# Hosted modulation pieces: one copy and one fold for each batch of up to ten

## The reference, cut to what matters

```python
for i in range(DEPTH):
    m_l = (jax.nn.silu(c) @ mod_w + mod_b)[:, None, :]
    m_c = jax.nn.silu(c_ctx) @ mod_w + mod_b
    sh1_l, sc1_l, g1_l, sh2_l, sc2_l, g2_l = jnp.split(m_l, 6, axis=-1)
    ...
    p_lat = _ada(x, norm1, sh1_l, sc1_l) @ w_in
    ... even_mixer or odd_mixer ...
    x = x + g1_l * (o_l.astype(x.dtype) @ w_out)
    x = x + g2_l * _sq_relu_mlp(_ada(x, norm2, sh2_l, sc2_l), mlp_w1, mlp_w2)
```

## Time and profile before

| | us |
|---|---|
| time, median of 3 runs | 2031.5 |
| lowest and highest | 2029.34, 2032.51 |
| span of the profiled execution | 2027.8 |

### The profile page before, as it was taken

The page is one execution under the profiler, slowest core; times in us unless marked ns, Lnnn a source line. Parts: engine busy times, 40 slices in busy tenths (PEclk is TensorE's granted clock), DMA queues, the critical chain, the costliest instruction groups (busy, mean ns, idle before and its releaser), DMA issues. The chain is left out here.

```text
span 2027.8 us, 42258 instructions
## 1 busy us (share of the span) xinstructions
PE 1853.9 (91%) x18096; PEld 1620.7 (80%) x18096; DVE 1252.8 (62%) x2170; ACT 858.4 (42%) x1588; POOL 291.0 (14%) x341
## 2 busy tenths in 40 slices
PE   7999877776899999999999799999889999889997
PEld 5787546656669888888978689999589999679997
DVE  4574785575567532543675778745668756667753
ACT  4321676345334221221435445534555345554432
POOL 0202204215131000003001321012030012021001
PEclk8999988979999999999999889999999999989998
DMA  9752840020243232323420166554136455225543
GB/s 314 204 179 83 276 161 4 4 64 5 68 143 101 87 104 83 104 83 104 125 83 1 49 197 191 188 188 155 56 108 195 155 188 187 84 84 186 187 150 102
DMA packets 249005, 255.04 MB, mean 126 GB/s; under 512 B 6914, under 2 KB 247187, under 8 KB 248691
## 3 DMA queue, kind: packets, MB, share of 16 engines
q1 hardware_dynamic: 239214, 242.85, 37.1%
q10 hardware_dynamic: 8740, 8.51, 1.3%
q0 software_dynamic: 864, 0.98, 0.3%
HBM read 251.28 MB, written 1.05 MB: 124 GB/s over the span
## 5 line engine op out<-in xcount | busy, mean ns | idle before, releaser
L529 DVE TENSOR_TENSOR RING_rounded<-RING,SC_rounded 128x1024 fp32r<-128x1024 f32 (+2 forms) x390 | 462.2, 1228 | 225.4 <-ACT SC_rounded L522 225.1
L549 PE MATMUL bank<-OT_rounded,SC_rounded 128*128 128x256 f32 (+1 forms) x1808 | 575.8, 318 | 14.5 <-DVE HT_rounded L1115 6.8
L550 PE MATMUL bank<-HT_rounded,SC_rounded 128*128 128x256 f32 (+1 forms) x1808 | 570.4, 316 | 0.0
L551 PE MATMUL bank<-OT_rounded,RING_rounded 128*128 128x256 f32 (+1 forms) x1808 | 568.9, 315 | 0.0
L522 ACT ACTIVATE SC_rounded<-RING 128x1024 fp32r<-128x1024 f32 (+2 forms) x390 | 372.6, 1006 | 327.6 <-DMA RING<-in_l_mlp_w 183.6
L549 PEld LDWEIGHTS bank<-OT_rounded,SC_rounded 128*128 128x128 f32 x1808 | 343.4, 190 | 44.9 <-DVE HT_rounded L1115 7.6
L551 PEld LDWEIGHTS bank<-OT_rounded,RING_rounded 128*128 128x128 f32 x1808 | 342.7, 190 | 25.4
L550 PEld LDWEIGHTS bank<-HT_rounded,SC_rounded 128*128 128x128 f32 x1808 | 343.1, 190 | 21.7
L549 PE MATMUL bank<-PT_rounded,SC_rounded 128*128 128x256 f32 (+1 forms) x896 | 277.5, 310 | 4.9 <-DVE RING_rounded L529 4.9
L550 PE MATMUL bank<-PT_rounded,SC_rounded 128*128 128x256 f32 (+1 forms) x896 | 276.5, 309 | 0.0
L551 PE MATMUL bank<-PT_rounded,RING_rounded 128*128 128x256 f32 (+1 forms) x896 | 275.9, 308 | 0.0
(11 more groups left out here) (570 smaller groups left out, 2807.4 us busy)
## 6 DMA issues: line engine op xcount, KB each, us to landing
RING<-in_l_mlp_w SPq DMA_DIRECT2D x64, 1024.0 KB, 5.2
RING<-in_w_ffn_in SPq DMA_DIRECT2D x44, 1024.0 KB, 5.1
RING<-in_l_mod_w SPq DMA_DIRECT2D x32, 1024.0 KB, 5.5
RING<-in_l_w_in SPq DMA_DIRECT2D x25, 1024.0 KB, 6.4
RING<-in_w_ffn_out SPq DMA_DIRECT2D x16, 768.0 KB, 4.3
RING<-in_w_in SPq DMA_DIRECT2D x10, 1024.0 KB, 5.3
RING<-in_w_ffn_out SPq DMA_DIRECT2D x16, 640.0 KB, 3.9
PT<-in_l_mod_w SPq DMA_DIRECT2D x8, 1024.0 KB, 9.9
```

What stands on the lines that cost most here:

```text
L529: net.nc.vector.tensor_tensor(low, whole, net.high4(s, m)[:, 0:self.w.kts[s], :].bitcast(F32), ALU.subtract).then_inc(self.split_ready, 1)
L549: net.nc.tensor.matmul(bank[:, tokens], high, x_high, start=start, stop=False)
L550: net.nc.tensor.matmul(bank[:, tokens], high, x_low, start=False, stop=False)
L551: return net.nc.tensor.matmul(bank[:, tokens], low, x_high, start=False, stop=stop)
```

## The change

Several pieces now add into the same bank before one copy and one fold. The two conditions lie in a new tile `net.COND` of 8 x 50 columns, zero elsewhere, at columns 18 and 19. `window(i)` is a slice of 32 columns of it in which the conditions stand at columns 2i and 2i+1. With the slice of place i as the stationary operand, piece i of a batch adds its sums to rows 2i and 2i+1 of each group of 32 and zeros to the others. `start` is set on the batch's first matmuls only, `stop` on its last. The constant of `fold` grows from 2 to 20 columns, of which a fold uses two for each piece.

`plan` cuts the pieces of a stage into equal batches of up to ten: 9 and 10 in attention, and 6, 3 and 4 in the others. `copy` and `fold` now go by batches. In attention the copy of the first batch stands on ScalarE's queue at the unit after the one that hosts its last piece, and `exps(0)` and `exps(1)` have no copy ahead of them. In the other three stages the one copy is the last thing on ScalarE. `biases` takes the place of `bias` in the four hosting stages. Its columns are ordered otherwise, so it issues two adds for each batch and layer: six in attention (batch 1 has pieces of both layers), two in each other stage. The first stage keeps its own code, and `bias` for its pieces 8 to 15. The constants after the fold's move by 18 columns.

```diff
+MOD_BATCH = 10
+C_OVER = C_FOLD + 2 * MOD_BATCH
...
+        self.COND = sb("COND", [P, KT, 32 + 2 * (MOD_BATCH - 1)])
...
-        self.c = net.SC[:, 8440:8696].rearrange("p (t m) -> p t m", m=32)
+        self.c = self.window(0)
...
-    def add(self, pe, n, first):
-
-        if n > first:
-            self.fold(pe, n - 1, first)
-        s = n % SLOTS
+    def window(self, i):
+
+        at = 2 * (MOD_BATCH - 1 - i)
+        return self.net.COND[:, :, at:at + 32]
+
+    def plan(self, first, last):
+
+        count = -(-(last + 1 - first) // MOD_BATCH)
+        ends = [first + (last + 1 - first) * n // count for n in range(count + 1)]
+        self.done += len(self.batches)
+        self.batches = [range(a, b) for a, b in zip(ends, ends[1:])]
...
+    def add(self, pe, n):
+
+        b, s = self.batch(n), n % SLOTS
+        slots = self.batches[b]
+        if n == slots[0] and b:
+            self.fold(pe, b - 1)
         pe.wait_ge(self.net.ring_loaded[s], 16 * (n // SLOTS + 1) + self.base[s])
         for i in range(2):
             for j in range(4):
                 kt, group = 4 * i + j, slice(32 * j, 32 * j + 32)
-                last = self.nc.tensor.matmul(self.sums[group, :], self.c[:, kt, :],
-                                             self.net.RING[:, s, SW * kt:SW * kt + SW], start=(i == 0), stop=(i == 1))
+                last = self.nc.tensor.matmul(self.sums[group, :], self.window(n - slots[0])[:, kt, :],
+                                             self.net.RING[:, s, SW * kt:SW * kt + SW], start=(n == slots[0] and i == 0),
+                                             stop=(n == slots[-1] and i == 1))
         last.then_inc(self.summed, 1)
 
-    def copy(self, act, n):
-        act.wait_ge(self.summed, n + 1)
-        if n:
-            act.wait_ge(self.folded, n)
+    def copy(self, act, b):
+        act.wait_ge(self.summed, self.batches[b][-1] + 1)
+        if b:
+            act.wait_ge(self.folded, self.count(b - 1))
         act.activation(self.rows, self.sums, ACT.Copy).then_inc(self.copied, 1)
 
-    def fold(self, pe, n, first):
-        pe.wait_ge(self.copied, n + 1)
+    def fold(self, pe, b):
+        pe.wait_ge(self.copied, self.count(b))
+        count = 2 * len(self.batches[b])
         for m in range(2):
-            last = self.nc.tensor.matmul(self.columns[:, 2 * (n - first) + m, :], self.rows[:, P * m:P * m + P],
-                                         self.net.const(C_FOLD, 2), start=True, stop=True)
+            last = self.nc.tensor.matmul(self.batch_columns[:, b, m, 0:count], self.rows[:, P * m:P * m + P],
+                                         self.net.const(C_FOLD, count), start=True, stop=True)
         last.then_inc(self.folded, 1)
...
+    def biases(self, dve):
+
+        half = self.ALL // 2
+        dve.wait_ge(self.folded, self.count(len(self.batches) - 1))
+        for slots in self.batches:
+            b = self.batch(slots[0])
+            for some in (range(slots[0], min(slots[-1] + 1, half)), range(max(slots[0], half), slots[-1] + 1)):
...
-            pool.memset(mod.c, 0.0).then_inc(zeroed, 1)
+            pool.memset(net.COND[:, :, :], 0.0).then_inc(zeroed, 1)
...
-            mod.copy(act, ahead[0])
             exps(0)
-            mod.copy(act, ahead[1])
             exps(1)
-            mod.copy(act, ahead[2])
             for u, (h, q) in enumerate(units):
                 k0 = first_key(q) * P
-                for n in hosted[u - 1] if u else ():
-                    mod.copy(act, n)
+                for b, slots in enumerate(mod.batches):
+                    if u and slots[-1] in hosted[u - 1]:
+                        mod.copy(act, b)
...
-            mod.copy(act, first_slot)
             kr = mem.kr.rearrange("p t c n m -> p (t c) n m")
             act.wait_ge(cum_ready, 1)
             act.activation(kr[:, :, 1, :], flat(mem.cum), ACT.Exp, scale=-DECAY).then_inc(exped, 1)
-            mod.copy(act, first_slot + 1)
             act.activation(flat(mem.bd), flat(mem.cum), ACT.Exp, scale=DECAY).then_inc(exped, 1)
-            mod.copy(act, first_slot + 2)
             act.wait_ge(cum_ready, 2)
             act.wait_ge(rate_used, 1)
             act.activation(kr[:, :, 0, :], flat(mem.sig), ACT.Exp, scale=-DECAY).then_inc(exped, 1)
```

More of the change, by code:

```diff
@@ L418, in __init__ @@
         self.columns = net.ps[7][:, 256:512].rearrange("p (t n) -> p t n", n=2)
+        self.batch_columns = net.ps[7][:, 256:512].rearrange("p (b m n) -> p b m n", m=2, n=32)
+        self.batches, self.done = [], 0
         self.base = list(net.ring_base)
@@ L465, in bias @@
+    def bias(self, dve, first, last):
+        dve.wait_ge(self.folded, last + 1)
+        count, layer = 2 * (last + 1 - first), 2 * first // 48
         at = COL[f"l{layer}_mod_b"] + 2 * first - 48 * layer
-        return self.nc.vector.tensor_tensor(self.net.MOD[:, 2 * first:2 * last + 2, :], self.columns[:, of:of + count, :],
+        return self.nc.vector.tensor_tensor(self.net.MOD[:, 2 * first:2 * last + 2, :], self.columns[:, 0:count, :],
                                             self.net.PAR[:, at:at + count].unsqueeze(2).to_broadcast([P, count, 2]),
@@ L2701, in _ @@
                 for n in hosted[u]:
-                    mod.add(pe, n, first_slot)
+                    mod.add(pe, n)
             weigh(len(units) - 1)
-            mod.fold(pe, last_slot, first_slot)
+            mod.fold(pe, len(mod.batches) - 1)
         @st.scalar
@@ L2739, in _ @@
                     act.activation(f, f, ACT.Copy, scale=net.DER[:, 14 + t:15 + t]).then_inc(damped, 1)
-            for n in hosted[-1]:
-                mod.copy(act, n)
+            mod.copy(act, len(mod.batches) - 1)
         @st.vector
@@ L2783, in _ @@
             nc.vector.tensor_copy(net.OT[:, 3, :], net.ps[6][:, :])
-            for some in ((first_slot, 23), (24, last_slot)):
-                mod.bias(dve, (first_slot, last_slot), *some)
+            mod.biases(dve)
 def load_log_exp(net, act):
@@ L3104, in _ @@
             act.activation(mem.far, mem.far, ACT.Exp, scale=-DECAY)
-            for n in range(first_slot + 2, last_slot + 1):
-                mod.copy(act, n)
+            mod.copy(act, 0)
         @st.vector
@@ L3439, in _ @@
                                  stop=True).then_inc(gate_ready, 1)
[L3440 to L3441 removed]
+                mod.add(pe, first_slot + t)
+            mod.fold(pe, len(mod.batches) - 1)
         @st.scalar
@@ L3453, in _ @@
                                                        for t in range(4)])
-            for n in range(first_slot, last_slot + 1):
-                mod.copy(act, n)
+            mod.copy(act, 0)
         @st.vector
```

47 lines of the change are left out of this document (27 added, 20 removed).

## The result

The changed kernel took 2014.4 us (median of 6 runs, 2009.4 to 2017.4), the kernel before 2030.2 (6 runs, 2028.8 to 2032.5). The ratio is 0.9926, with a 95% interval of 0.9913 to 0.9939: 15 us faster, where I had forecast 9.8. The profiled execution took 2013.0 us with a span of 2011.1, so some 1.9 us lie outside the span. Against the 2027.8 of the earlier trace rows the span is 16.7 us shorter.

A forecast was written before the change was run, and what follows sets the result against it. It saw TensorE busy in most of a 2027.8 us span. Attention 5.8, rwkv_prepare 3.2, rwkv_back_decay -0.1 and rwkv_finish 0.9 made 9.8 us, taken off the median 2031.5: 2021.7 us, range 2017.0 to 2027.5.

The forecast's parts named there:

- the term for attention's start: Start of attention: three adds without copies and folds between let score(2) start earlier; gain 3.2 us, between 2.0 and 3.7.
- what lies outside the hosting stages: Stages that host no pieces: no gain or loss counted, 0 us.
- since the clock fell at about the second add: Attention's start: reason for taking score(2) at 205.4, between 204.9 and 206.6, with the first add beginning at 201.7.
- my upper bound: Attention's start: score(2) at 204.9 at the earliest, from 201.7 + 3 x 1.07; gain at most 3.7 us.
- Attention's units: Attention after its start: fewer folds on TensorE, 0.64 us per four units; gain 3.0 us, between 1.5 and 5.5.
- The biases: End of attention: four more bias adds on VectorE cost 0.4 us, between 0.2 and 0.8.
- `rwkv_prepare`: Copies no longer hold up ScalarE's last wide exponential, 2.6 us earlier; stage gains 3.2 us, between 2.0 and 3.7.
- Chunks 0: Stage behind rwkv_prepare: a worse clock phase costs about 1 us, but counted as 0 since the clock is already low.
- rival (b): Clock phase: three stages behind a host start with longer half-clock stretches, 2 us each; 3.8 us net, 2027.7; chance 0.09.
- `rwkv_back_decay` and `rwkv_finish`: First loses 0.1 us for a bias add; second gains 0.9 us from an earlier last fold, between 0 and 1.0.
- Rival (c): Slower loads: shifted slices load three times as long, an add takes some 1.8 us for 1.07; 2041 us; chance 0.05.
- Rival (a): Filler only: start at half clock, half the folds hidden, prepare at its lower bound; 4.6 us net, 2026.9; chance 0.10.

The follow-up runs named there:

- a_again: The changed kernel run once more, unaltered, for a second profile; ratio 0.9946 to the kernel before.
- e4_batched_pad64: The changed kernel with an unused tile of 64 bytes per partition behind CONST; ratio 0.9930 to the kernel before.
- g_all: All batches as in the changed kernel, but folded columns written in the old order, with the old bias adds; ratio 0.9941 to the kernel before.
- x_exps_first: The kernel before with exps(0) and exps(1) moved ahead of the copies of pieces 16 and 17 on ScalarE; ratio 1.0002.
- b_again: The kernel before run again, unchanged, for a second profile; ratio 0.9993.
- g_start: The kernel before with the changed kernel's layout and only attention's three pieces ahead (16 to 18) batched; ratio 0.9954.
- e1: The kernel before with the changed kernel's memory layout and nothing else; ratio 0.9999.
- e2: The kernel before with an unused tile of 64 bytes per partition behind CONST, so only addresses move; ratio 0.9987.
- g_prep: The kernel before with the changed kernel's layout and only the six pieces of rwkv_prepare batched; ratio 0.9990.
- x_warm_start: The kernel before with four unused identity matmuls on TensorE between score(1) and the add of piece 16; ratio 0.9988.
- h_warm: g_all plus unused identity matmuls at the ends of rwkv_prepare (three) and rwkv_back_decay (four); 2011.7 us, ratio 0.9924 to the kernel before.

## Why the prediction was wrong, point by point

**The whole.** The four kernels with all batches and no filler (changed, a_again, e4_batched_pad64, g_all) have ratios of 0.9926, 0.9946, 0.9930 and 0.9941. Weighted by their intervals that is 0.9936, a gain of 13.0 us give or take 1.5 if the four are taken as independent (a_again and g_all share their runs of the kernel before), for 9.8 forecast. The 15.8 us between the first two medians are at the high end: in the second set the changed kernel's median was 1.6 us higher (2016.0 for 2014.4) and that of the kernel before 2.4 us lower (2027.8 for 2030.2). Two steps of the prediction failed: the term for attention's start, 3.2 us, was too small, and what lies outside the hosting stages was put at 0.

**Attention's start: the first step that failed.** I had 3.2 us, bounds 2.0 and 3.7. In the pair of profiles the turn went from 12.3 to 7.4 us, 4.9. By the table it takes 12.7 us on average in the seven kernels with neither its batch nor the filler, and 8.1 in the six with it: 4.6 us. The mechanism was right: TensorE's waits for copies go, and ScalarE's order is worth nothing (x_exps_first). The size was wrong in three places. First, "since the clock fell at about the second add": I kept that fall for the changed kernel and took 3.7 us from the first add to score(2). It took 2.73, at full clock. Second, my upper bound was three adds at full clock, but it added 1.07 us three times, 3.2 us, where adds that follow one another take 2.80 us for three. Third, it ended at score(2). From there to the transposition it was 1.2 us at half clock and is 0.6 at full.

At full clock on both sides (b_again against the changed kernel) the turn gains only 10.2 - 7.4 = 2.8 us; the other 1.8 of the 4.6 come from the clock. The clock fell during the turn in six of those seven profiles, for 5.5 to 10.0 us, and in two of the six with the batch (g_start, e4), for 3.4 us each; in those two the turn took 9.3, in the four others 7.4 to 7.5. The Trainium skill ("TensorE: Matmul & The Clock Gate", part 1) says that activity releases the throttle. I had read that against the change alone, as filler work taken away. Here the folds were followed by waits, and the adds now stand closer together. That this is what keeps the clock up agrees with the counts and with the 2.80 us for three adds, but no run shows it apart from chance: the kernel before kept the clock up once as well.

**Attention's units: right in mechanism, somewhat large in size.** Four units take 14.7 us for 15.4, 0.66 less where I had 0.64, and VectorE is what is late, as said. Units with the end: 59.9 us on average in six unbatched kernels (before, b_again, e1, e2, x_exps_first, g_prep) and 57.8 in the three with the new bias adds: 2.1 for 3.0 - 0.4 = 2.6. Without e1 and x_exps_first, whose units took some 1.5 us longer than the others', it is 1.6, and in the first pair 1.8. The biases cost 0.26 (0.55 for six adds, 0.29 for two in the earlier trace rows), not 0.4, so the folds gave 1.9 to 2.4, not 3.0.

**`rwkv_prepare`: right in this pair, somewhat larger on average.** 3.3 us for 3.2. The wide exponential comes 2.7 us earlier in the stage (26.6 for 29.3 us; forecast 2.6), and the fold is what is late, 0.62 us, with VectorE next. The average over all profiles without a filler here is 46.3 us unbatched against 42.2 batched: 4.1. The length again goes with the clock. Where 13.7 of the stage's first 16.5 us run at half clock, it is 47.4 (b_again, e1) against 44.2 (g_all), and otherwise 44.8 to 46.5 against 41.6 to 41.7.

**Chunks 0: the term set to zero.** 104.4 us on average behind an unbatched prepare, 105.3 behind a batched one: 0.9 us given back. This is rival (b) at half its price. The clock is what differs: the stage has 13 us at half clock on average where prepare is batched, and 4.4 where it is not. The longer idle time ahead that the rival named shows in the stage's head (5.1 to 5.9 us at half clock in four of those five, 3.0 to 3.6 in seven of the eight others, 5.8 in the eighth). The larger part lies in stretches later in the stage, and why the clock falls there is open. Single profiles of one side differ by up to 3.8 us here, so the safer figure is that of prepare and chunks 0 together: 150.7 against 147.5 us, 3.2.

**`rwkv_back_decay` and `rwkv_finish`: right.** +0.1 for +0.1, and -0.9 for -0.9.

**Rival (c)** is refuted: loads out of shifted slices take 117 ns for 118, an add 1.07 us. **Rival (a)** too: the start ran at full clock in four of the six kernels with its batch, and the folds were on the path.

**The sum.** By the averages: 7.1 (attention, 72.6 in the six kernels without its batches or the filler against 65.5 in the five with both) + 4.1 - 0.9 - 0.1 + 0.9 = 11.1 us in the stages that the change reaches. Of the 1.3 us above the forecast, the start gives 1.7 (12.7 against 7.8 in these five), the units -0.4, prepare 0.9, chunks 0 -0.9. Up to the 13.0 us of the times 1.9 are left.

**Outside: the second step that failed.** I counted the phase of the clock at 0, and the fast end of the range, 2017.0, left 1 us for it beyond the sum of my upper bounds (13.5 us, or 2018.0). The first stage and what lies behind the first MLP's start gave 7.3 us in the pair. This was not the chance of these two executions alone: the second profiles, a_again and b_again, differ there by 6.9 us. Two things show in it.

The first is the layout. The first stage took 196.4 to 197.6 us in the four kernels with the tiles at their old places (before, b_again, x_exps_first, x_warm_start) and 193.8 to 196.2 in the ten where they are shifted. With the same 10.2 us at half clock in it, it is 196.6 against 195.2. From the first MLP's start to the first scan the four took 527.4 to 528.5 us with 10.1 to 11.9 of them at half clock, and four of the ten 525.9 to 527.2 with 11.7 to 14.5. The second MLP takes back 1 us (256.5 to 257.0 against 257.4 to 259.4). An estimate from these is 2 us in all, and the times of e1_layout and e2_pad64 (0.2 and 2.6 us) allow that.

The second is the clock. The other six of the ten kernels (e2, g_prep, changed, a_again, e4, h_warm) had only 6.3 to 7.2 us at half clock between the first MLP's start and the first scan, and took 521.3 to 523.8 us. The first profile of the kernel before was at half clock for 73.6 us behind the first MLP's start, that of the changed kernel for 55.4. This makes the last column fall in two groups, 1451.0 to 1452.2 and 1455.1 to 1456.3. Both occur with batches (four short, one long) and without (three short, six long), so batching does not fix the group. Whether it makes the short one more likely is open: with 14 profiles, chance can't be excluded. The clocks of all runs bear on it. Among runs of one kernel, a mean granted clock that is higher by 0.01 goes with a time that is some 8 us shorter (188 runs). Runs of the five kernels that batch attention's start without a filler had a mean clock of 0.968 to 0.969, the runs of the kernel before in the first two groups 0.966; by that slope, an estimate, 2 to 3 us of the gain go with the clock, attention's own share of it included.

## What to carry to other kernels

Ask of each short matmul group behind a wait not only what it costs, but what clock it runs at, and whether that follows from the wait. Where a wait in a dense stretch goes, the gain can be larger than the wait, since more of the stretch then runs at full clock (here 4.6 us on average for 2.8 at full clock on both sides); what is gained ahead of a stage can be partly given back in it, by the clock. And where a stage's length varies by 2 us from one execution to the next, take the stage's price from several profiles of several kernels, and give the range room on both sides: one pair of profiles put 7.3 us, nearly half the difference, into stretches whose work the change leaves alone. A change that adds a tile also moves others: run the old kernel with the new layout before a difference elsewhere is put down to the change.

## What the runs showed of the hardware

A shift of the tiles behind CONST by 64 and by 128 bytes changed the rate of full-clock matmuls whose weights come from SC and the ring: 859, 864 and 871 in 200 us of the first MLP, so 0.6 and 1.4% faster. For the 864 (e2_pad64) the program differs in nothing else; the 871 are those of e4_batched_pad64, which has the batches too. In a stretch of the second MLP, with a half as wide moving operand, the same 64 bytes made it 0.6% slower, 855 against 850 in 100 us. Over the whole kernel little of it is left (ratios 0.9999 and 0.9987 for e1_layout and e2_pad64). Which pair of operands meets there was not tried.

The granted clock took both of its levels in the same program at the same place: 0.50 and 1.00 at attention's start in two executions of the kernel before, worth 2.1 us there. Over the whole kernel, among runs of the same program, 0.01 of mean granted clock went with some 8 us of time (188 runs, clocks of 0.959 to 0.974).
